# Gate halves combined before the P7 split, and the first weight sum made by a second load and an adding transfer

## What is computed

```
def gated_conv_ffn(x, w_gate, w_up, conv_w, conv_b, w_down):
    g = jnp.einsum('bsd,df->bsf', x, w_gate)
    g = causal_dwconv3(g, conv_w) + conv_b
    up = jnp.einsum('bsd,df->bsf', x, w_up)
    return jnp.einsum('bsf,fd->bsd', jax.nn.silu(g) * up, w_down)
```

## Time and profile before

| | us |
|---|---|
| median of 3 runs | 1761.76 (1760.08 to 1763.84) |
| the profiled execution, its time | 1763.11 |
| its span, first to last instruction | 1761.4 |
| PE busy | 1698.8 |
| DVE busy | 1120.4 |
| ACT busy | 896.1 |
| POOL busy | 663.2 |

### The profile page before, as it was taken

The page is one execution under the profiler, slowest core; times in us unless marked ns, Lnnn a source line. Parts: engine busy times, 40 slices in busy tenths (PEclk is TensorE's granted clock), DMA queues, the critical chain, the costliest instruction groups (busy, mean ns, idle before and its releaser), DMA issues.

```text
span 1761.4 us, 29505 instructions
## 1 busy us (share of the span) xinstructions
PE 1698.8 (96%) x9907; PEld 1479.0 (84%) x9907; DVE 1120.4 (64%) x1967; ACT 896.1 (51%) x1685; POOL 663.2 (38%) x735
## 2 busy tenths in 40 slices
PE   7999999999999999999989999999999989999998
PEld 6788889999878888888879999888788879999887
DVE  6677767777763334674598888433356698888332
ACT  6666766666652233433455666322363556666222
POOL 4555665655520001000256777011004277775000
PEclk9999999999999999999999999999999999999999
DMA  4112123233323334133364554433232455544332
GB/s 137 52 47 61 51 59 75 74 85 78 78 72 95 95 108 127 56 97 98 108 132 114 126 120 114 128 99 102 86 95 72 124 122 121 123 120 110 100 97 90
DMA packets 293265, 169.39 MB, mean 96 GB/s; under 512 B 13391, under 2 KB 282578, under 8 KB 293170
## 3 DMA queue, kind: packets, MB, share of 16 engines
q1 hardware_dynamic: 281714, 148.69, 29.6%
q0 software_dynamic: 11264, 19.15, 6.8%
q10 hardware_dynamic: 192, 0.33, 0.1%
HBM read 147.02 MB, written 2.16 MB: 85 GB/s over the span
## 4 chain that ended last, share of the span: by engine, by line
PE 64%; DVE 17%; issue 9%; ACT 7%; POOL 1%; DVEq 0%; ACTq 0%; DMA 0%; POOLq 0%
PE ps L411 38%; PE ps L2569 10%; DVE w_split L2629 4%; PE ps L1027 3%; PE ps L3053 2%; PE ps L877 2%; ACT w_split L2623 1%; DVE tmp L1370 1%; DVE w_split L368 1%; DVE arena_r L1375 1%; PE ps L890 1%; DVE ps L2894 1%; PE ps L856 1%; ACT tmp L1098 1%; PE ps L835 1%
## 5 line engine op out<-in xcount | busy, mean ns | idle before, releaser
L411 PE MATMUL ps<-arena_r,w_split 128*128 128x512 f32 x1854 | 425.2, 390 | 1.8 <-POOL w_split L366 1.5
L411 PEld LDWEIGHTS ps<-arena_r,w_split 128*128 128x128 f32 x1854 | 347.2, 188 | 77.1 <-POOL w_split L366 1.9
L411 PE MATMUL ps<-u,w_split 128*128 128x512 f32 x1641 | 400.6, 396 | 0.0
L368 DVE TENSOR_TENSOR w_split<-w_raw,w_split 128x1024 fp32r<-128x1024 f32 x149 | 182.3, 1224 | 297.4 <-ACT w_split L352 297.2
L352 ACT CAST w_split<-w_raw 128x1024 fp32r<-128x1024 f32 (+4 forms) x249 | 213.3, 874 | 305.9 <-PE ps L411 265.1
L411 PEld LDWEIGHTS ps<-u,w_split 128*128 128x128 f32 x1641 | 304.4, 189 | 63.3 <-issue 0.5
L2569 PE MATMUL ps<-xs_u,w_split 128*128 128x256 f32 x1728 | 229.0, 286 | 24.4 <-DVE tmp L2956 16.5
L2569 PEld LDWEIGHTS ps<-xs_u,w_split 128*128 128x128 f32 x1728 | 215.0, 192 | 32.5 <-DVE tmp L2956 14.9
L1978 POOL TENSOR_TENSOR tmp<-tmp 128x512 f32<-128x512 f32 x33 | 46.7, 1415 | 261.2 <-ACT tmp L1934 232.5
L1975 POOL COPY tmp<-tmp 128x512 f32<-128x512 f32 x5 | 3.2, 645 | 352.6 <-ACT tmp L1934 186.9
L366 POOL TENSOR_TENSOR w_split<-w_raw,w_split 128x256 fp32r<-128x256 f32 x168 | 123.0, 764 | 23.7 <-ACT w_split L352 23.7
(11 more groups left out here) (335 smaller groups left out, 2799.1 us busy)
## 6 DMA issues: line engine op xcount, KB each, us to landing
w_raw<-in_w_in_dram SPq DMA_DIRECT2D x118, 256.0 KB, 3.2
w_raw<-in_w_ffn_down_dram SPq DMA_DIRECT2D x64, 256.0 KB, 3.1
w_raw<-in_w_ffn_gate_dram SPq DMA_DIRECT2D x52, 256.0 KB, 3.3
w_raw<-in_w_ffn_up_dram SPq DMA_DIRECT2D x52, 256.0 KB, 3.1
w_raw_b<-in_w_ffn_up_dram SPq DMA_DIRECT2D x36, 256.0 KB, 3.9
w_raw_b<-in_w_ffn_gate_dram SPq DMA_DIRECT2D x36, 256.0 KB, 3.3
w_raw<-in_w_in_even_dram SPq DMA_DIRECT2D x32, 256.0 KB, 3.1
w_raw<-in_w_in_odd_dram SPq DMA_DIRECT2D x32, 256.0 KB, 3.2
```

The lines of the kernel that those rows point to most:

```text
L368: ins = eng.tensor_tensor(lo, r, hi, ALU.subtract)
L411: last = pe.matmul(out_ap, w_tile(c, ws, k - n0), moving(k, ms), start=start and n == 0, stop=stop and n == len(total) - 1, skip_group_che ...
```

## The change

In each period DVE now does the two gate additions before the split for P7, where they stood behind it. `first_sum` is no longer a tensor operation: SP loads u1 a second time, into `e_sum`, and POOL issues a transfer that adds u2 onto it. `third_sum` then needs no finished `e`, since it overwrites only the first copy; `second_sum` waits for the adding transfer. In the stretch where the plain tiles end, ACT casts the weights of the first P1 and P2 earlier, and the input x for P4 is made later, inside the first period. The rename of the semaphore `e_bc` lies elsewhere and changes no work.

```
-LOADS = {"u1": "up", "u2": "up", "g1": "g1", "g2": "g2"}
+LOADS = {"u1": "up", "e": "up", "u2": "up", "g1": "g1", "g2": "g2"}
...
-            per = 32 if part == "up" else 16
+            per = 48 if part == "up" else 16
...
-            for name in ("u1", "u2", "g1", "g2"):
+            for name in ("u1", "e", "u2", "g1", "g2"):
...
-                    else:
+                    elif name != "e":
                         low_split(sp, layer, i, gs - 1, OF_LAST[name == "g2"])
...
-                if kind in ("p5", "p6"):
-                    act.wait_ge(sem("summed_w"), summed_to(layer, i, gs, 1 if kind == "p5" else 2))
+                if kind == "p6":
+                    act.wait_ge(sem("summed_w"), summed_to(layer, i, gs))
                 else:
-                    act.wait_ge(sem("third_sum" if kind == "p7" else "fourth_sum"), added_to(layer, i, gs))
+                    act.wait_ge(sem({"p5": "first_sum", "p7": "third_sum", "p3": "fourth_sum"}[kind]), added_to(layer, i, gs))
...
             plain_unit(7)
+            act_seventh(act, layer, 0, *ORDER[0])
+            act_seventh(act, layer, 0, *ORDER[1])
             act_x(act, layer, "p6")
             plain_hi(2)
-            act_seventh(act, layer, 0, *ORDER[0])
             tap(3)
-            act_seventh(act, layer, 0, *ORDER[1])
             act_x(act, layer, "p7")
             silu(3)
             act_seventh(act, layer, 0, *ORDER[2])
-            act_x(act, layer, "p4")
...
             def first_sum(i, gs):
                 loaded(pool, layer, i, gs, "up")
-                if not (isinstance(i, int) and gs < PLAIN + 2):
-                    low_split(pool, layer, i, gs - 2, 5)
-                    pool.wait_ge(sem("summed_w"), summed_to(layer, i, gs - 2, 2))
-                pool.tensor_tensor(quarter(layer, gs, "e"), quarter(layer, gs, "u1"), quarter(layer, gs, "u2"), ALU.add) \
-                    .then_inc(sem("summed_w"), 1)
+                pool.dma_start(quarter(layer, gs, "e"), quarter(layer, gs, "u2"), accum_op=ALU.add) \
+                    .then_inc(sem("first_sum"), 16)
 
             def third_sum(i, gs):
                 loaded(pool, layer, i, gs, "g1")
-                pool.wait_ge(sem("summed_w"), summed_to(layer, i, gs, 1))
...
                 low_split(pool, layer, i, gs, 0)
+                pool.wait_ge(sem("first_sum"), added_to(layer, i, gs))
                 pool.wait_ge(sem("third_sum"), added_to(layer, i, gs))
...
                 lo_ahead(i, fs, 2)
-                lo_ahead(i, fs, 3)
                 if not carried:
+                    dve_x(dve, layer, "p4")
                     plain_low(PLAIN - 1)
                     dve_x(dve, layer, "p3")
                 if carried:
                     add_gate_right(i, fs - 1)
                 if begun:
                     add_gate_left(i, fs)
+                lo_ahead(i, fs, 3)
```

More of the change, by code:

```diff
@@ L2200, in pe_even @@
                     pe.wait_ge(sem("diagonal"), 2)
-                    pe.matmul(bank(7), ones[:], sq[:, 0, :], start=True, stop=True).then_inc(sem("e_bc"), 1)
+                    pe.matmul(bank(7), ones[:], sq[:, 0, :], start=True, stop=True).then_inc(sem("e_row"), 1)
             w_ready(pe, EZ + 2)
@@ L2249, in act_even @@
             hi()
-            act.wait_ge(sem("e_bc"), 1)
-            act.copy(rbc[:, 0, :], bank(7)).then_inc(sem("e_rbc"), 1)
+            act.wait_ge(sem("e_row"), 1)
+            act.copy(rbc[:, 0, :], bank(7)).then_inc(sem("e_row"), 1)
             hi()
@@ L2371, in dve_even @@
             lo()
-            dve.wait_ge(sem("e_rbc"), 1)
+            dve.wait_ge(sem("e_row"), 2)
             link(dve.tensor_tensor(r2, r, r, ALU.mult))
@@ L2442, in split_slot, with summed_to @@
             return wsp[:, (FIRST["ffn", layer] + n // 2) % 2, part, n % 2 * QUARTER:(n % 2 + 1) * QUARTER]
-        SUMMED = (1, 2)
         COMBINED = ("gate_left", "up_right", "gate_right")
-        def summed_to(layer, i, gs, which):
-            return num(2 * (N_PAIR * layer + gs - PLAIN) + SUMMED.index(which) + 1, i, 8)
+        def summed_to(layer, i, gs):
+            return num(N_PAIR * layer + gs - PLAIN + 1, i, 4)
         def added_to(layer, i, gs):
@@ L2509, in load_pair @@
                     sp.wait_ge(sem("w_lo"), t + 2 * PLAIN - (1 if name == "u1" else 0))
-                w, half = (gate if name[0] == "g" else up), int(name[1]) - 1
+                w, half = (gate if name[0] == "g" else up), 1 if name[1:] == "2" else 0
                 src = (w[:, col:col + P] if isinstance(col, int) else w[:, bass.ds(col, P)]) \
@@ L2792, in period @@
                 if not carried:
+                    act_x(act, layer, "p4")
                     plain_hi(PLAIN - 1)
@@ L2847, in fourth_sum @@
                 low_split(pool, layer, i, gs, 4)
-                pool.wait_ge(sem("summed_w"), summed_to(layer, i, gs, 2))
+                pool.wait_ge(sem("summed_w"), summed_to(layer, i, gs))
                 pool.dma_start(quarter(layer, gs, "g2"), quarter(layer, gs, "g1"), accum_op=ALU.add) \
@@ L2938, in dve_ffn @@
             seventh_low(dve, layer, 0, *ORDER[2])
-            dve_x(dve, layer, "p4")
             def add_up_right(i, gs):
```

## The result

The changed kernel takes 1806.17 us (median of 3 runs, 1802.70 to 1811.19) against 1761.76 before: a ratio of 1.0254, interval 1.0212 to 1.0297. It is slower, where 1732 was forecast. Its profiled execution took 1802.7 us, with a span of 1801.0 us.

What follows compares the result with a forecast made beforehand. PE was taken to set the pace, with 28.2 us of waits to get back. From 1763.1 us, 25 for these and 5 at the plain tiles left 1733, a median of about 1732; range 1727 to 1752.

Steps and rivals of the forecast that it cites:

- What bounded the kernel before: Seven-product part: PE sets the pace, DVE close behind; seven products take 10.0 us, and small PE waits remain.
- The P5 gaps: PE's waits ahead of P5 for `add_gate_right`, held up by DVE's P7 split: 28 waits, 16.5 us in all.
- So the move costs nothing while the split ends by then: P7 split behind both gate additions ends by 967.3, when PE wants it; cover at least 0.1 us, normally 1.2.
- blocked past the time PE wants it: Sign of being wrong: the P7 split behind the gate additions is itself blocked too long for PE; no size given.
- The issue itself does not hold DVE: POOL's transfer issue, 0.85 us, leaves DVE's P7 split free to end 0.55 us after the sum, as elsewhere.
- B: Rival: POOL's chain falls behind PE; 0.3 to 0.5 us a period return, 1744 to 1751 us; chance 0.21.
- Its second way: A POOL issue waits for a DVE split beside it, two issues of up to 0.7 us each; chance 0.05.
- D: Rival: longer DMA landings make POOL's P1 split late every period; about 1783 us, likelier near 1770; chance 0.12.
- C: Rival, no gain: gaps move from P5 to P4 or P1 in full; 1758 to 1765 us; chance 0.07.
- The transfer: First sum by transfer: P5 split 1.56 to 0.7 us, DMA 8.5 of 10.0 us a period, all hidden behind PE.
- Where the plain tiles end: Earlier casts, later x for P4 and a shorter DVE split save 2.5 us a layer, 5 us; bounds 0 and 10.
- A: Main case: all the predicted gains hold within 6 us, 1727 to 1741 us; chance 0.60.

Runs made afterwards that it cites:

- e1: Kernel before with only DVE's order changed, both gate additions ahead of the P7 split: 1778.39 us, ratio 1.009.
- e5: Changed kernel with two POOL waits: its P1 split waits for DVE's P7 split, its second sum for DVE's P4 split: 1732.91 us, ratio 0.9834.
- e2: Changed kernel with the P7 split ahead of the gate additions again: 1763.15 us, ratio 1.0002.
- e4: Changed kernel with one more wait, POOL starting its P1 split only after DVE's P7 split: 1755.87 us, ratio 0.9959.
- m1: Separate kernel, one DVE subtraction beside POOL trains of additions: at most 1.71 us; in a mix with an adding transfer's issue, up to 5.02 us.
- m2: Separate kernel, DVE subtraction beside issue then three additions: 4.97 to 3.28 us when held; issue last: at most 1.74; POOL waiting behind the issue (`wait`): 0.68.
- e10: e1 with the fourth sum a tensor operation, so POOL issues no transfer in the periods: 1752.85 us, ratio 0.9962.
- e9: e1 with both POOL waits of e5, first sum still a tensor operation: 1741.96 us, ratio 0.9888.
- e8: e5 with the stretch where the plain tiles end as in the kernel before: 1734.61 us, ratio 0.9846.
- e7: Changed kernel with only one wait, POOL's second sum waiting for DVE's P4 split: 1761.76 us, ratio 1.0011.

## Why the prediction was wrong

**What bounded the kernel before: right.** The P5 gaps were there to be had. In the changed kernel and in e1 they are gone, and in e5 the periods are the 10.0 us that the prediction worked out from one product's 1.43. e5's profiled execution, 1731.83 us, is 31.3 us below that of before; with about 4 of them at the plain tiles (see below), some 27 are the gaps, of 28.2 that the prediction counted and 25 that it took.

**The step that failed: "So the move costs nothing while the split ends by then".** It put the P7 split's end at 966.1, "or 967.2 if POOL's P1 split (966.14 before) gets in first". That is a hold by one POOL operation, and even for one the figure is too low: by the prediction's own rows DVE ends 0.55 us after POOL, and the P1 split ended at 967.70, so with the 0.44 us by which it may come earlier DVE would end at 967.8, past the 967.3 at which PE wants it. The cover of "at least 0.1" us was not there. Measured are 5.2 to 6.0 us in 13 periods, until the end of all that POOL had in its train: third sum, issue, two splits, second sum. e2 against the changed kernel shows that the loss, 43 us, needs this split in its new place, and e1, where the P7 split starts at the same point of the third sum and is free with its end, that it needs the issue ahead of the third sum as well; e4, with one wait on POOL, that it goes through POOL; m1, m2 and e10 that an issue has to stand ahead for a hold to outlast one operation. The prediction did name a P7 split "blocked past the time PE wants it" among its signs of being wrong, but gave it neither a price nor a chance. The 39.6 us of the profile are 26.8 us more idle time and 12.8 us of slower matmuls behind it; the prediction had no term for the second.

**"The issue itself does not hold DVE": true as it stands, and wrong for the sum.** m2's `wait` trials bear it out (0.68 us beside an issue). In the earlier trace rows the P7 split had started before the only issue of the period, and so ended with the third sum. In the changed kernel it starts behind an issue, the first sum's, which the change itself put in front of the third sum. In m1 that is the difference of 0.68 and 5.02 us. The prediction priced the issue by its duration, and not by what stands behind it.

**B had the right row and the wrong rule.** The 3.15 us of the earlier trace rows were laid to a late third sum. e1 has this length in 27 splits, in the period shown with the third sum 0.17 us behind the first: the P4 split falls into the block from the fourth sum's issue on. Why it was rare before shows in one row of the kernel before, the second of POOL's two splits in the period of the earlier trace rows:

```profile
968.19 1.29 POOL L2629 TENSOR_TENSOR w_split<-w_raw,w_split 128x512 fp32r<-128x512 f32 x1 [0.49 <-ACT w_split L2623]
```

In every period from 957 to 1086 us POOL idles 0.41 to 0.49 us there for ACT's cast, which waits for `add_gate_right` by way of the tap. That gap ends the block, and the P4 split behind it (969.00) takes 1.02 us. Two periods of the kernel before lack the gap (at 1493.06 and 1569.26), and they are the two with a P4 split over 3 us, 3.15 and 3.21; the prediction knew the first alone. With the additions earlier ACT is in time (in e1 the same cast is over at 1001.70, before POOL's first split is), the gap is gone and the block reaches the second sum. In the changed kernel itself B hardly came: three P4 splits of 3.1 to 3.3 us, 4.2 us of waits for `add_up_right`. Where it did, in e1, its 11 to 18 us were too small: 28.3 us at P4. Its second way, an issue that waits for a DVE split, is not there: the 31 issues of e1 that have a held split beside them take 0.85 to 0.88 us.

**D had the sign and not the mechanism.** The slow side was to come from landings lengthened by over 1.7 us. Adding transfers landed in 3.3 to 3.8 us against 3.9, loads in 3.1 to 3.4, and e5 ran at a DMA share of 0.81 without a gap, its transfers and loads landing in 3.2 to 4.1 us. **C**, the gap that moves to P4 with no gain, is what e2 does (ratio 1.0002), and not the changed kernel; it had 0.07.

**The transfer: right in size of work, hidden as forecast.** P5 split at 0.683 us, DMA share 0.81, e2 not slower than before. Its worth showed only behind the waits: 7 us, e9 against e8.

**Where the plain tiles end: 4 us where 5 were taken.** In e5 P7 of the first pair starts at 919.44 against 921.68, and in the second layer 1.8 us sooner after the last plain unit. In the first layer 1.2 us of it are the last plain unit's own wait, 0.44 against 1.66 us: DVE's split of twice the width takes 1.21 us with the first sum off POOL, as foretold, against 2.84. The moved casts may be about 1.7 (e8's median, not clear of noise; in its trace P7 of the first pair comes 1.2 and 1.3 us later after the last plain unit than in e5's).

**The sum as such** came true in another kernel: the edits of the change bring 1732.9 us (e5), 1732 was forecast, once POOL waits twice per period. That it is so near is in part luck, 27 and 4 us in place of 25 and 5. A slip in the range changes nothing: A's "within 6 us" is 1726 to 1738 around 1732, not 1727 to 1741.

The Trainium skill, page "SBUF — State Buffer", section "SBUF: two separate sides", says of the lock between DVE and GpSimd that whoever starts first holds it for the whole instruction. The trains without an issue agree (DVE in at the next boundary, at most 1.71 us in m1); for what follows an issue the hold can be longer than one instruction (3.28 to 4.97 us over three additions in m2), and there the measurement decides.

**Open.** Why an issue ties what follows is not shown, only that none of these splits and trials was held past the end of a POOL operation without one, and that a wait undoes it. Nor is the rule complete. In m1 and m2 all ten trials that start 0.12 to 0.58 us after an issue, and so ahead of the next addition, are held to the end of the train. In the kernels most splits that start there run free: 49 of them in the changed kernel, e2 and e7 take 0.68 us, though the third sum begins 0.61 to 0.82 us after that issue; only the six of the first pairs are held, for 2.2 us, to the end of the third sum. All 13 long ones start later, inside the third sum. What sets the two apart was not found. How small a gap is enough is not known either: ahead of the third sum 0.70 us from issue to operation were held and 0.75 were not (three cases), behind the fourth sum's issue 1.00 still was (e4). Who wins when both engines already follow themselves closely was not tried.

## What to carry to other kernels

Price a DVE operation with two SBUF inputs, at the worst, by POOL's whole train behind the last transfer that POOL issued, not by the one operation that it meets; a long tail of its durations (maximum against median) is the sign, and its ends lie 0.55 to 0.57 us behind the end of a train. Before moving such an operation, write down what POOL runs from there on without waiting, and if a train is in the way, let POOL wait for the operation: two waits brought 73 us here, where their engine had the time to spare. A gap taken from the bounding engine also takes gaps from the others, so a pattern that was rare before may become the period.

## What the hardware showed that was not expected

- Behind an adding transfer that POOL issues, POOL's next tensor operations, if they follow without a gap, can hold a DVE subtraction with both inputs in SBUF until the last of them has ended: 4.97 down to 3.28 us for three additions (m2), 5.2 to 6.0 us in the changed kernel. Without the issue it is at most 1.71 us (m1), with the issue last 1.74, with a wait behind the issue 0.68, and with one input in PSUM 0.68.
- A wait of PE of 3.92 us was followed by a granted clock of 0.64 over the next 3.95 us; over the whole span PE's busy time rose by 12.8 us, nearly half of the added idle time itself, and the mean granted clock fell from 0.996 to 0.986.
- The fourth sum's issue takes 0.85 to 0.88 us in the kernel before and in e1, with or without a DVE split held beside it. In the changed kernel it takes 0.99 to 1.19 us in the 28 periods in which it starts 1.84 to 2.03 us after the first sum's issue did, and 0.85 to 0.88 us where it starts 2.16 us or more after it.
